# Reordering the stage between a projection and a mix: channel transform first, layer-norm sums among the time transform's parts

## The chip, the cores and the metric

The kernel runs on one core of one Trainium2 chip. The metric is the device time of one execution in microseconds (us), the median over the runs of the same program. All engine times below come from one profiled execution of it, in us from the start of its span.

## What is computed

The program is a transformer block (sliding-window attention and a squared-ReLU MLP), followed by a second model part of two layers on 1024 tokens and a context of 256. The change lies in the even layer of the second part, `_even_mix`, which all 1280 tokens pass:

```python
def _fourier_mix(v, fw):
    b, l, _ = v.shape
    vg = v.reshape(b, l, B_GROUPS, B_GROUP_DIM).astype(jnp.float32)
    f = jnp.fft.fftn(vg, axes=(1, 3), norm='ortho').real.astype(v.dtype)
    return jnp.einsum('blgd,gde->blge', f, fw).reshape(b, l, B_WIDTH)

def _even_mix(h, w_in, a_conv_w, a_conv_b, a_ln_g, a_ln_b, a_pw_w, a_pw_b, b_fw, w_out):
    a_val, a_glu, a_gate, b_val, b_gate = _split(h @ w_in, [A_WIDTH, A_WIDTH, A_WIDTH, B_WIDTH, B_WIDTH])
    u = a_val * jax.nn.sigmoid(a_glu)
    u = jax.nn.silu(_layernorm(_dwconv(u, a_conv_w) + a_conv_b, a_ln_g, a_ln_b))
    y_a = (u @ a_pw_w + a_pw_b) * jax.nn.silu(a_gate)
    y_b = _fourier_mix(b_val, b_fw) * jax.nn.silu(b_gate)
    return jnp.concatenate([y_a, y_b], axis=-1) @ w_out
```

`_dwconv` is a depthwise convolution of 31 taps. The Fourier transform over channels and time is done as matrix products.

## The kernel before, in words

Everything is float32. Each operand of a product is split into a rounded high part and a remainder, and `mm3` (lines 159 to 161) makes three matmuls out of one product: high by high, high by low, low by high. Activations lie with channels on the 128 partitions and tokens along the free side, in tiles of 512, 512 and 256 tokens (`TILES2`). Weights come as units of 512 KB through three slots: SyncE loads unit u once TensorE has begun unit u-2 (`load_unit`, line 138), ScalarE writes its high part (`split_hi`, line 149), VectorE its low part (`split_lo`, line 154). Each engine works through its own list strictly in the written order and waits on semaphores. A stage is a block; all engines meet at its end.

The even projection (the block that begins at line 1134) has 20 units of output channels. TensorE makes a unit's three tiles, ScalarE takes them out of PSUM (line 1152), and VectorE puts the convolution's taps between its other work: `taps(n, chunks)` issues `n` steps `conv_out = conv_in * w + conv_out` over 1295 columns (line 1252), in turn over the four channel chunks, 124 in all. The last four units are the Fourier branch: VectorE folds them (`fold`, lines 1222 to 1227), ScalarE writes `bH`, VectorE `bL` (`fold_low`, lines 1231 and 1232). ScalarE may take the next unit out only after `fold_low` of the last one.

The next block (from line 1310 on) is the stage of the change. Its jobs before the change, in TensorE's order:

- **Means:** 12 matmuls with a matrix of ones sum `conv_out` over channels (line 1333), three tiles by four chunks. VectorE subtracts the mean (`centred`, line 1478), ScalarE squares (line 1429, four buffers).
- **Channel transform:** ten blocks `z` of 12 matmuls each (`bH`, `bL` by `cdsH`, `cdsL`), in two pairs of banks in turn. ScalarE writes `zH` (line 1438), VectorE `zL` (line 1482). After each block one matmul sums squares (`square_sum`, line 1340).
- **Time transform:** four parts over the odd outputs, 24 matmuls of 512 columns each, then three halves of 48 matmuls of 256 columns each. Their outputs, `fH` and `fL`, are written by ScalarE (line 1463) and VectorE (line 1502) in four groups of four, alternating. The weights `wH`, `wL` are here constants of the transform.
- Beside it, the layer norm goes on: square root (ScalarE, line 1444), reciprocal (VectorE, line 1487), scaling by it (line 1491), silu and its high part (ScalarE, lines 1450 and 1452), low part (VectorE, line 1496). Each change between square root and silu on ScalarE has an `ACT_TABLE_LOAD`.
- **Mix:** 24 jobs of products with the Fourier weights and the pointwise weights, begun when `f_lo` is 16, each multiplied by its gate (lines 1521, 1523, 1468, 1510).

The waits that tie the time transform to the others, before:

```python
                    if half == 0:
                        pe.wait_ge(ln_rms, 3)
                    if half == 2:
                        pe.wait_ge(f_lo, 8)
```

## Time and profile before

| | us |
|---|---|
| median of 3 runs (lowest, highest) | 2329.1 (2325.64, 2332.3) |
| the profiled execution | 2324.8 |
| its span | 2323.0 |
| even projection's last matmul starts | 1444.58 |
| stage of the change, first matmul | 1460.06 |
| its channel transform starts | 1470.97 |
| its time transform starts | 1493.88 |
| its mix starts | 1539.62 |

TensorE (PE) is busy for 93% of the span, VectorE (DVE) for 56%, ScalarE (ACT) for 32%. The stage of the change is about 120 us of it. A line of the timeline gives start, duration, engine, source line and operation, output and inputs, and in brackets how long the engine sat idle before it and what released it. A matmul's duration is longer than the step to the next one, since they are pipelined; steps are read from the starts.

### The profile page before, as it was taken

The page shows a single profiled execution, that of the slowest core. Times are in us where ns is not written, and L with a number is a line of the kernel's source. Part 1 is how long each engine was busy: PE and PEld are TensorE (multiplying, and loading weights), DVE is VectorE, ACT ScalarE, POOL GpSimd, SP SyncE. Part 2 cuts the span into 40 slices and gives each one's busy share as a digit, 9 for nine tenths or more (in the row PEclk, how much of TensorE's full clock was granted, in tenths as well). Part 3 has the DMA queues.
Part 4 walks back from the last instruction along what each step waited for, and adds up shares of the span by engine and source line. Part 5 has one row for each costly group of instructions (what it writes and reads, how often), then busy time and mean ns, then how long its engine had stood idle before and what let it go on. Part 6 is the DMA issues. An engine that isn't in the chain of part 4 may idle for free. (4 is left out here: it accounts for less than half of the span.)

```text
span 2323.0 us, 25481 instructions
## 1 busy us (share of the span) xinstructions
PE 2159.5 (93%) x10132; PEld 1757.6 (76%) x10132; DVE 1299.4 (56%) x2157; ACT 733.4 (32%) x1366; POOL 196.4 (8%) x162
## 2 busy tenths in 40 slices
PE   5988989999999999999889998889989999879896
PEld 4876668788888888888578887678867788756675
DVE  6248853762462462464678888773354233478734
ACT  4236632420220220222441211651252211156522
POOL 2003310100000000000010000000020000044401
PEclk9978899999999999999989999899999999879998
DMA  4100021221221221221201231133121211100032
GB/s 152 55 19 1 1 91 55 106 103 54 98 102 55 99 101 55 100 100 55 109 28 37 71 91 39 51 102 138 40 119 46 82 46 55 36 5 15 10 118 82
DMA packets 42742, 157.95 MB, mean 68 GB/s; under 512 B 4224, under 2 KB 8960, under 8 KB 41344
## 3 DMA queue, kind: packets, MB, share of 16 engines
q1 hardware_dynamic: 40176, 146.49, 18.7%
q10 hardware_dynamic: 2448, 9.84, 1.1%
q8 instruction: 80, 1.31, 0.2%
q14 instruction: 38, 0.31, 0.0%
HBM read 136.39 MB, written 19.92 MB: 67 GB/s over the span
## 5 line engine op out<-in xcount | busy, mean ns | idle before, releaser
L159 PE MATMUL banks<-u2H,wH 128*128 128x512 f32 x736 | 291.6, 396 | 14.1 <-POOL u2L L355 5.0
L160 PE MATMUL banks<-u2L,wH 128*128 128x512 f32 x736 | 288.2, 392 | 0.0
L161 PE MATMUL banks<-u2H,wL 128*128 128x512 f32 x736 | 287.8, 391 | 0.0
L159 PE MATMUL banks<-uH,wH 128*128 128x512 f32 x672 | 262.8, 391 | 1.6 <-DVE uL L355 1.2
L154 DVE TENSOR_TENSOR wL<-raw,wH 128x1024 fp32r<-128x1024 f32 x153 | 186.8, 1222 | 138.3 <-ACT wH L149 138.3
L160 PE MATMUL banks<-uL,wH 128*128 128x512 f32 x672 | 262.4, 391 | 0.0
L161 PE MATMUL banks<-uH,wL 128*128 128x512 f32 x672 | 262.4, 390 | 0.0
L159 PE MATMUL banks<-aH,wH 128*128 128x512 f32 x640 | 249.7, 390 | 2.0 <-PEq L181 2.0
L160 PE MATMUL banks<-aL,wH 128*128 128x512 f32 x640 | 249.8, 390 | 0.0
L161 PE MATMUL banks<-aH,wL 128*128 128x512 f32 x640 | 249.7, 390 | 0.0
L149 ACT CAST wH<-raw 128x1024 fp32r<-128x1024 f32 x153 | 159.6, 1044 | 273.4 <-DMA raw<-in_wstream 268.5
L1252 DVE SCALAR_TENSOR_TENSOR conv_out<-conv_in,par,conv_out 128x1295 f32<-128x1295 f32 x120 | 180.3, 1562 | 0.6
L159 PEld LDWEIGHTS banks<-u2H,wH 128*128 128x128 f32 x736 | 139.1, 189 | 49.6 <-issue 16.0
L161 PEld LDWEIGHTS banks<-u2H,wL 128*128 128x128 f32 x736 | 139.0, 189 | 29.4
L160 PEld LDWEIGHTS banks<-u2L,wH 128*128 128x128 f32 x736 | 139.3, 189 | 28.8 <-issue 1.2
L1032 DVE TENSOR_TENSOR h<-banks,h 128x512 f32<-128x512 f32 x64 | 43.9, 689 | 206.6 <-PE banks L161 206.6
L159 PEld LDWEIGHTS banks<-uH,wH 128*128 128x128 f32 x672 | 126.8, 189 | 31.4 <-issue 5.1
L161 PEld LDWEIGHTS banks<-uH,wL 128*128 128x128 f32 x672 | 126.7, 189 | 26.5
L160 PEld LDWEIGHTS banks<-uL,wH 128*128 128x128 f32 x672 | 126.7, 189 | 26.2
L159 PEld LDWEIGHTS banks<-aH,wH 128*128 128x128 f32 x640 | 120.6, 188 | 27.4 <-issue 2.4
L161 PEld LDWEIGHTS banks<-aH,wL 128*128 128x128 f32 x640 | 120.6, 188 | 25.2
L160 PEld LDWEIGHTS banks<-aL,wH 128*128 128x128 f32 x640 | 120.4, 188 | 25.0
(277 smaller groups left out, 3802.0 us busy)
## 6 DMA issues: line engine op xcount, KB each, us to landing
raw<-in_wstream SPq DMA_DIRECT2D x153, 512.0 KB, 3.5
mod_w<-in_mod_w SPq DMA_DIRECT2D x48, 512.0 KB, 5.4
x_scratch<-h SPq DMA_DIRECT2D x2, 4096.0 KB, 11.3
gt<-gates_scratch SPq DMA_DIRECT2D x8, 640.0 KB, 4.1
h<-in_x SPq DMA_DIRECT2D x4, 1024.0 KB, 10.6
h<-in_x SPq DMA_DIRECT2D x1, 4096.0 KB, 13.4
h<-x_scratch SPq DMA_DIRECT2D x1, 4096.0 KB, 12.3
xo<-x_scratch SPq DMA_DIRECT2D x1, 4096.0 KB, 13.4
```

Of the source, the lines that this page charges most:

```text
L149: act.copy(wH[:, u % R, :], raw[:, u % R, :]).then_inc(weights_hi, 1)
L154: eng.tensor_tensor(wL[:, u % R, :], raw[:, u % R, :], wH[:, u % R, :].bitcast(F32), ALU.subtract)\
L159: first = pe.matmul(out, aH, bH, start=start, stop=False)
L160: pe.matmul(out, aH, bL, start=False, stop=False)
L161: return first, pe.matmul(out, aL, bH, start=False, stop=stop)
L1032: dve.tensor_tensor(dst, bank(4 + s * 2 + ti), dst, ALU.add).then_inc(down_drained, 1)
L1252: dve.scalar_tensor_tensor(dst, src, w, dst, ALU.mult, ALU.add).then_inc(conv_step, 1)
```

## The change

The taps: of the last two steps of the projection, the one that issued all taps that were left (11) now issues 4. The seven left over are issued in the next stage, four and three, between the splits of two weight units. `taps` moves out of the block and takes the engine as an argument. TensorE starts the stage with the channel transform; the means stand ahead of part `tc == 3` of the time transform and wait for all 124 taps; the square sums stand behind the groups of that part and of the first two halves. On ScalarE all twelve squares stand together ahead of the first group of outputs, and the square root and silu of each token tile stand between groups of outputs; on VectorE accordingly. Halves wait on other semaphores, some banks change.

```diff
@@ -1260,11 +1261,11 @@
                         if v < 8 and v % 2:
                             product(v // 2)
                         split_lo(dve, E0 + v + 2)
-                        taps(7, min((v + 1) // 2, HALF))
+                        taps(dve, 7, min((v + 1) // 2, HALF))
                     else:
                         fold(v - 16)
                         split_lo(dve, E0 + v + 2)
-                        taps(4 if v < 18 else HALF * TAPS, HALF)
+                        taps(dve, 4 if v < 19 else 0, HALF)
                         fold_low(v - 16)
...
@@ -1286,7 +1287,7 @@
...
-        Z_BANKS, MEAN_BANKS = (6, 0), (2, 5, 4)
+        Z_BANKS, MEAN_BANKS, SQ_BANKS = (6, 0), (1, 3, 5), (4, 5, 2)
...
-        ODD, MOD2, MOD0 = (6, 7, 2, 0), (4, 5), (1, 3)
+        ODD, MOD2, MOD0 = (6, 7, 2, 0), (1, 3), (6, 7)
...
@@ -1328,16 +1329,21 @@
...
-                for ti, (c0, n) in enumerate(STILES):
-                    for c in range(HALF):
-                        m = pe.matmul(bank(MEAN_BANKS[ti], n), ones[:], conv_out[:, c, c0:c0 + n], start=c == 0, stop=c == HALF - 1)
-                    m.then_inc(sum_done, 1)
+                def means():
+                    pe.wait_ge(conv_step, HALF * TAPS)
+                    for ti, (c0, n) in enumerate(STILES):
+                        for c in range(HALF):
+                            m = pe.matmul(bank(MEAN_BANKS[ti], n), ones[:], conv_out[:, c, c0:c0 + n], start=c == 0, stop=c == HALF - 1)
+                        m.then_inc(sum_done, 1)
+
...
                 def square_sum(j):
                     ti, c = jobs[j]
                     if j == HALF:
                         pe.wait_ge(centred, len(jobs))
+                    if j == 2 * HALF:
+                        pe.wait_ge(f_lo, 3)
                     pe.wait_ge(ln_sq_ready, j + 1)
-                    pe.matmul(bank(3 + ti, TILES2[ti][1]), ones[:], sq[:, j % LN_SQ, 0:TILES2[ti][1]], start=c == 0,
+                    pe.matmul(bank(SQ_BANKS[ti], TILES2[ti][1]), ones[:], sq[:, j % LN_SQ, 0:TILES2[ti][1]], start=c == 0,
                               stop=c == HALF - 1).then_inc(ln_sq_used, 1)
 
...
@@ -1351,10 +1357,6 @@
                             f.then_inc(units_begun, 1)
                         if g % 2:
                             m.then_inc(z_done, 1)
-                    if z >= 1:
-                        square_sum(z - 1)
-                for j in range(ZC - 1, len(jobs)):
-                    square_sum(j)
...
@@ -1362,6 +1364,8 @@
                     return u % R
                 D0 = W0["dft"]
                 for tc in range(4):
+                    if tc == 3:
+                        means()
                     slot = begin(D0 + tc)
...
@@ -1375,13 +1379,14 @@
                                 f.then_inc(units_begun, 1)
                         if tc == 3:
                             m.then_inc(dft_done, 1)
+                            square_sum(g)
                 for half in range(3):
                     u = D0 + 4 + min(half, 1)
                     slot = begin(u) if half < 2 else u % R
                     if half == 0:
-                        pe.wait_ge(ln_rms, 3)
-                    if half == 2:
-                        pe.wait_ge(f_lo, 8)
+                        pe.wait_ge(centred, 2 * HALF)
+                    else:
+                        pe.wait_ge(f_lo, (2, 8)[half - 1])
                     for g in range(HALF):
                         for tc in range(2):
                             for part in range(2):
@@ -1394,6 +1399,8 @@
                                 if g == 0 and tc == 0 and part == 0 and half < 2:
                                     f.then_inc(units_begun, 1)
                         m.then_inc(dft_done, 1)
+                        if half < 2:
+                            square_sum(HALF * (half + 1) + g)
 
                 for j, (_, _, bias, ti) in enumerate(mjobs):
                     oc, (c0, n) = j // 3, TILES2[ti]
...
@@ -1408,6 +1415,7 @@
                         pe.wait_ge(s_lo, len(jobs))
                     if j < 6:
                         pe.wait_ge(f_lo, 16)
+                        pe.wait_ge(ln_rms, 3)
                     else:
                         pe.wait_ge(mix_v, j - 5)
...
@@ -1428,41 +1436,57 @@
                         act.wait_ge(ln_sq_used, j - LN_SQ + 1)
                     act.activation(sq[:, j % LN_SQ, 0:n], conv_out[:, c, c0:c0 + n], ACT.Square).then_inc(ln_sq_ready, 1)
 
-                for s in range(2):
-                    act.wait_ge(gate_stored[s], 16 * 5)
-                for j in range(LN_SQ):
-                    square(j)
...
+                def root(ti):
+                    n = STILES[ti][1]
+                    act.wait_ge(ln_sq_used, (ti + 1) * HALF)
+                    act.activation(rs[:, TILES2[ti][0]:TILES2[ti][0] + n], bank(SQ_BANKS[ti], n), ACT.Sqrt, bias=eps[:, 0:1],
+                                   scale=1.0 / 512).then_inc(ln_rms, 1)
+
...
                 for z in range(ZC):
                     for half in range(2):
                         act.wait_ge(z_done, 2 * z + half + 1)
                         act.copy(zH[:, z, TN * half:TN * half + TN], bank(Z_BANKS[z % 2] + half)).then_inc(z_hi, 1)
-                    if z >= 1 and z - 1 + LN_SQ < len(jobs):
-                        square(z - 1 + LN_SQ)
-                split_hi(act, W0["dft"] + 2)
-                for ti, (c0, n) in enumerate(STILES):
-                    act.wait_ge(ln_sq_used, (ti + 1) * HALF)
-                    act.activation(rs[:, TILES2[ti][0]:TILES2[ti][0] + n], bank(3 + ti, n), ACT.Sqrt, bias=eps[:, 0:1], scale=1.0 / 512)\
-                        .then_inc(ln_rms, 1)
-                for j, (ti, c) in enumerate(jobs):
-                    c0, n = STILES[ti]
-                    v = conv_out[:, c, c0:c0 + n]
-                    act.wait_ge(ln_v, j + 1)
-                    act.activation(v, v, ACT.Silu, bias=pcol("ln_b", c)).then_inc(ln_silu, 1)
-                    act.wait_ge(ln_silu, j + 1)
-                    act.copy(sH[:, c, c0:c0 + n], v).then_inc(s_hi, 1)
-                    if j == 5:
-                        split_hi(act, W0["dft"] + 3)
+                    if z == 5:
+                        split_hi(act, W0["dft"] + 2)
+                split_hi(act, W0["dft"] + 3)
+                for s in range(2):
+                    act.wait_ge(gate_stored[s], 16 * 5)
                 split_hi(act, W0["dft"] + 4)
+                for j in range(len(jobs)):
+                    square(j)
+                spectrum(0)
                 split_hi(act, W0["dft"] + 5)
-                for j, (b, o, n, g, dst, scale) in enumerate(fjobs):
-
-
-                    act.wait_ge(dft_done, j + 1 if j < 4 or g % 2 else j + 2)
-                    if j >= 4 and g % 2:
-                        act.wait_ge(f_lo, j)
-                    act.activation(dst(fH, g), banks[:, b, o:o + n], ACT.Copy, scale=scale).then_inc(f_hi, 1)
-                    if j in (3, 7, 15):
-                        split_hi(act, W0["fw"] + (3, 7, 15).index(j))
+                root(0)
+                silu(0)
+                spectrum(4)
+                root(1)
+                silu(1)
+                split_hi(act, W0["fw"])
+                spectrum(8)
+                root(2)
+                silu(2)
+                split_hi(act, W0["pw"])
+                spectrum(12)
+                split_hi(act, W0["pw"] + 1)
                 for j, (yc, gc, bias, ti) in enumerate(mjobs):
                     act.wait_ge(mix_v, j + 1)
                     act.copy(tile_of(yH, yc, ti), gv[:, j % 3, 0:TILES2[ti][1]]).then_inc(y_hi, 1)
...
@@ -1471,38 +1495,64 @@
 
             @block.vector
             def _(dve):
...
                 split_lo(dve, W0["dft"] + 2)
-                for ti, (c0, n) in enumerate(STILES):
-                    dve.wait_ge(ln_rms, ti + 1)
-                    dve.reciprocal(rs[:, TILES2[ti][0]:TILES2[ti][0] + n], rs[:, TILES2[ti][0]:TILES2[ti][0] + n]).then_inc(ln_rstd, 1)
-                    dve.wait_ge(ln_rstd, ti + 1)
-                    for c in range(HALF):
-                        v = conv_out[:, c, c0:c0 + n]
-                        dve.scalar_tensor_tensor(v, v, pcol("ln_g", c), rs[:, TILES2[ti][0]:TILES2[ti][0] + n], ALU.mult, ALU.mult).then_inc(ln_v, 1)
+                taps(dve, 4, HALF)
                 split_lo(dve, W0["dft"] + 3)
-                for j, (ti, c) in enumerate(jobs):
-                    c0, n = STILES[ti]
-                    dve.wait_ge(s_hi, j + 1)
-                    dve.tensor_tensor(sL[:, c, c0:c0 + n], conv_out[:, c, c0:c0 + n], sH[:, c, c0:c0 + n].bitcast(F32),
-                                      ALU.subtract).then_inc(s_lo, 1)
+                taps(dve, HALF * TAPS, HALF)
+                for ti in range(2):
+                    centre(ti)
                 split_lo(dve, W0["dft"] + 4)
+                centre(2)
+                spectrum_low(0)
                 split_lo(dve, W0["dft"] + 5)
-                for j, (b, o, n, g, dst, scale) in enumerate(fjobs):
-                    dve.wait_ge(f_hi, j + 1)
-                    dve.scalar_tensor_tensor(dst(fL, g), banks[:, b, o:o + n], scale, dst(fH, g).bitcast(F32), ALU.mult,
-                                             ALU.subtract).then_inc(f_lo, 1)
-                    if j in (3, 7, 15):
-                        split_lo(dve, W0["fw"] + (3, 7, 15).index(j))
+                normalise(0)
+                spectrum_low(4)
+                normalise(1)
+                split_lo(dve, W0["fw"])
+                silu_low(0)
+                spectrum_low(8)
+                normalise(2)
+                silu_low(1)
+                split_lo(dve, W0["pw"])
+                spectrum_low(12)
+                silu_low(2)
+                split_lo(dve, W0["pw"] + 1)
 
```

`normalise(ti)` is the reciprocal and the four scalings of one tile, `silu_low(ti)` its four low parts, `spectrum_low(first)` the four `fL` of a group, `silu(ti)` four times silu and high part.

How the order moves, first on TensorE, at the third to fourth part of the time transform (`conv_out` by `ones` are the means, `wH` and `zH` the transform's operands):

```order
 L160 MATMUL banks<-wL,zH 128x512
 L161 MATMUL banks<-wH,zL 128x512
+L1336 MATMUL banks<-conv_out,ones 128x512 x8
+L1336 MATMUL banks<-conv_out,ones 128x256 x4
 L159 MATMUL banks<-wH,zH 128x512
 L160 MATMUL banks<-wL,zH 128x512
```

The 12 means are now behind 72 matmuls of the time transform instead of ahead of the channel transform, and the fourth part is behind them.

ScalarE before, from the last block of the channel transform on (`zH` is its high part, `ln_rs` the square root, `conv_out` the silu in place, `sH` its high part):

```order
L149 CAST wH<-raw 128x1024 [waits raw_loaded2]
L1444 ACT_TABLE_LOAD
L1444 ACTIVATE ln_rs<-banks,eps 128x512 [waits ln_sq_used] x2
L1444 ACTIVATE ln_rs<-banks,eps 128x256 [waits ln_sq_used]
L1450 ACT_TABLE_LOAD
L1450 ACTIVATE conv_out<-conv_out,par 128x512 [waits ln_v]
L1452 CAST sH<-conv_out 128x512 [waits ln_silu]
L1450 ACTIVATE conv_out<-conv_out,par 128x512 [waits ln_v]
```

and ScalarE of the change from the squares on (`ln_sq` squares, `fH` outputs of the time transform):

```order
L1437 ACTIVATE ln_sq<-conv_out 128x512 [waits ln_centred] x4
L1437 ACTIVATE ln_sq<-conv_out 128x512 [waits ln_sq_used,ln_centred] x4
L1437 ACTIVATE ln_sq<-conv_out 128x256 [waits ln_sq_used,ln_centred] x4
L1462 ACTIVATE fH<-banks 128x512 [waits dft_done] x4
L149 CAST wH<-raw 128x1024 [waits raw_loaded2]
L1442 ACT_TABLE_LOAD
L1442 ACTIVATE ln_rs<-banks,eps 128x512 [waits ln_sq_used]
L1450 ACT_TABLE_LOAD
L1450 ACTIVATE conv_out<-conv_out,par 128x512 [waits ln_v]
L1452 CAST sH<-conv_out 128x512 [waits ln_silu]
L1450 ACTIVATE conv_out<-conv_out,par 128x512 [waits ln_v]
L1452 CAST sH<-conv_out 128x512 [waits ln_silu]
```

The squares are no longer between the channel transform's blocks but in one row, each from the fifth on waiting for `ln_sq_used`, which TensorE's square sums raise; the first group of outputs stands behind them, then one tile's root and silu, and only then (three rows further) the second group of outputs. The same two table loads, root, silu and group follow twice more.

VectorE before, from the third tile's reciprocal on (`wL` weight unit's low part, `sL` low part of silu, `fL` low part of the outputs):

```order
L1487 RECIPROCAL ln_rs<-ln_rs 128x256 [waits ln_rms]
L1491 SCALAR_TENSOR_TENSOR conv_out<-conv_out,par,ln_rs 128x256 [waits ln_rstd]
L1491 SCALAR_TENSOR_TENSOR conv_out<-conv_out,par,ln_rs 128x256 x3
L154 TENSOR_TENSOR wL<-raw,wH 128x1024 [waits weights_hi]
L1496 TENSOR_TENSOR sL<-conv_out,sH 128x512 [waits ln_s_hi] x8
L1496 TENSOR_TENSOR sL<-conv_out,sH 128x256 [waits ln_s_hi] x4
L154 TENSOR_TENSOR wL<-raw,wH 128x1024 [waits weights_hi] x2
L1502 SCALAR_TENSOR_TENSOR fL<-banks,fH 128x512 [waits f_hi] x4
L154 TENSOR_TENSOR wL<-raw,wH 128x1024 [waits weights_hi]
L1502 SCALAR_TENSOR_TENSOR fL<-banks,fH 128x256 [waits f_hi] x4
```

and VectorE of the change, from the first group of outputs on:

```order
L1526 SCALAR_TENSOR_TENSOR fL<-banks,fH 128x512 [waits f_hi] x4
L154 TENSOR_TENSOR wL<-raw,wH 128x1024 [waits weights_hi]
L1509 RECIPROCAL ln_rs<-ln_rs 128x512 [waits ln_rms]
L1513 SCALAR_TENSOR_TENSOR conv_out<-conv_out,par,ln_rs 128x512 [waits ln_rstd]
L1513 SCALAR_TENSOR_TENSOR conv_out<-conv_out,par,ln_rs 128x512 x3
L1526 SCALAR_TENSOR_TENSOR fL<-banks,fH 128x256 [waits f_hi] x4
L1509 RECIPROCAL ln_rs<-ln_rs 128x512 [waits ln_rms]
L1513 SCALAR_TENSOR_TENSOR conv_out<-conv_out,par,ln_rs 128x512 [waits ln_rstd]
L1513 SCALAR_TENSOR_TENSOR conv_out<-conv_out,par,ln_rs 128x512 x3
L154 TENSOR_TENSOR wL<-raw,wH 128x1024 [waits weights_hi]
L1519 TENSOR_TENSOR sL<-conv_out,sH 128x512 [waits ln_s_hi] x4
L1526 SCALAR_TENSOR_TENSOR fL<-banks,fH 128x256 [waits f_hi] x4
```

Reciprocal and scaling of each tile now stand behind a group of `fL`, and a group of `fL` behind them, where before all three tiles were done ahead of all groups.

SyncE's list has the same transfers in the same order.

## Rows read from the trace of the kernel before

**Rows 1.** The page: engines over the span; DMA issues, KB each, us to landing.
```profile
PE 2159.5 (93%) x10132; PEld 1757.6 (76%) x10132; DVE 1299.4 (56%) x2157; ACT 733.4 (32%) x1366; POOL 196.4 (8%) x162
...
raw<-in_wstream SPq DMA_DIRECT2D x153, 512.0 KB, 3.5
```

**Rows 2.** Timeline of PE, 1444 to 1494: start us, us, instruction, [idle before <-releaser].
```profile
1444.58 0.28 PE L161 MATMUL banks<-u2Hc,wL 128*128 128x256 f32 x1
...
1460.06 11.26 PE L1333 MATMUL banks<-conv_out,ones 128*128 128x512 f32 x24 [15.20 <-PEq L1134]
...
1470.97 0.47 PE L159 MATMUL banks<-cdsH,bH 128*128 128x256 f32 x1
...
1478.62 1.02 PE L1340 MATMUL banks<-ln_sq,ones 128*128 128x512 f32 x2
...
1480.91 1.02 PE L1340 MATMUL banks<-ln_sq,ones 128*128 128x512 f32 x2
...
1492.34 1.89 PE L1340 MATMUL banks<-ln_sq,ones 128*128 128x256 f32 x8
```

**Rows 3.** Timeline of DVE around the end of the even projection.
```profile
1434.81 16.84 DVE L1252 SCALAR_TENSOR_TENSOR conv_out<-conv_in,par,conv_out 128x1295 f32<-128x1295 f32 x11
...
1454.55 0.69 DVE L1222 TENSOR_TENSOR bf<-bt 128x512 f32<-128x512 f32 x1 [1.43 <-ACT bt L1152]
...
1459.32 0.42 DVE L1232 TENSOR_TENSOR bL<-bt,bH 128x256 fp32r<-128x256 f32 x1
```

**Rows 4.** Timeline of ACT at the same place.
```profile
1453.16 1.36 ACT L1152 ACTIVATE bt<-banks 128x512 f32<-128x512 f32 x3 [18.01 <-DVE bL L1232]
```

**Rows 5.** Timeline of PE through the time transform, to the first mix matmul.
```profile
1493.88 0.59 PE L159 MATMUL banks<-wH,zH 128*128 128x512 f32 x1
...
1510.21 0.39 PE L161 MATMUL banks<-wH,zL 128*128 128x512 f32 x1
...
1512.83 0.79 PE L159 MATMUL banks<-wH,zH 128*128 128x512 f32 x1 [2.23 <-DVE wL L154]
...
1520.13 0.39 PE L159 MATMUL banks<-wH,zH 128*128 128x256 f32 x1
...
1537.38 0.28 PE L161 MATMUL banks<-wH,zL 128*128 128x256 f32 x1
...
1539.62 0.47 PE L159 MATMUL banks<-fH,wH 128*128 128x512 f32 x1 [1.96 <-DVE fL L1502]
```

**Rows 6.** Stretches: busy time of each engine, PEclk, DMA share, GB/s.
```profile
1514.00:1516.00 2.00, 2.00 (x7) 1.52 (x6) 2.00 (x4) 1.94 (x6) 0.00 (x0) 0.50 0.64 168
```

**Rows 7.** Timeline of DVE in the stage of the change.
```profile
1478.72 1.41 DVE L1482 TENSOR_TENSOR zL<-banks,zH 128x512 fp32r<-128x512 f32 x2 [0.88 <-ACT zH L1438]
...
1496.11 3.35 DVE L1487 RECIPROCAL ln_rs<-ln_rs 128x512 f32<-128x512 f32 x1 [0.78 <-ACT ln_rs L1444]
...
1499.49 2.74 DVE L1491 SCALAR_TENSOR_TENSOR conv_out<-conv_out,par,ln_rs 128x512 f32<-128x512 f32 x4
...
1512.69 6.25 DVE L1496 TENSOR_TENSOR sL<-conv_out,sH 128x512 fp32r<-128x512 f32 x12
...
1518.86 2.35 DVE L154 TENSOR_TENSOR wL<-raw,wH 128x1024 fp32r<-128x1024 f32 x2
```

**Rows 8.** Timeline of ACT in the stage of the change.
```profile
1494.09 1.28 ACT L1444 ACT_TABLE_LOAD   x1
...
1495.38 1.63 ACT L1444 ACTIVATE ln_rs<-banks,eps 128x512 f32<-128x512 f32 x3
...
1497.03 1.28 ACT L1450 ACT_TABLE_LOAD   x1
...
1500.28 0.73 ACT L1450 ACTIVATE conv_out<-conv_out,par 128x512 f32<-128x512 f32 x1 [1.96 <-DVE conv_out L1491]
...
1501.56 0.72 ACT L1450 ACTIVATE conv_out<-conv_out,par 128x512 f32<-128x512 f32 x1
...
1525.06 0.63 ACT L1463 ACTIVATE fH<-banks 128x256 fp32r<-128x256 f32 x1
...
1528.98 0.64 ACT L1463 ACTIVATE fH<-banks 128x256 fp32r<-128x256 f32 x1 [0.80 <-DVE fL L1502]
```

81 lines of the change are left out of this document (59 added, 22 removed).

## The prediction

> **What bounds the kernel now.** On the page TensorE is busy for 93% of the span [rows 1], so time is lost only where it waits. I read its timeline first, for gaps. The largest in this stretch lies before the stage of the change: the last matmul of the projection starts at 1444.58, the first of the stage at 1460.06, with 15.2 us idle in brackets [rows 2]. VectorE's timeline shows why: it issues 11 taps in a row from 1434.81, 16.84 us [rows 3]; ScalarE may not take out the last unit before, and its bracket shows 18.01 us of waiting [rows 4]; then fold and low part end at 1459.74, which is 1459.32 + 0.42 [rows 3]. Behind the gap TensorE makes the means, 10.91 us (1460.06 to 1470.97), and the channel transform with the squares, 22.91 us (to 1493.88) [rows 2, 5]. The time transform has three short gaps: 2.4 us before its fourth part, 0.2 before the halves, 2.1 before the mix (steps from the last start: 1510.21 to 1512.83, and 1537.38 to 1539.62, less one matmul) [rows 5]. Gaps up to the mix: 15.4 + 2.4 + 0.2 + 2.1 = 20.1 us. After a gap of 2.4 us the granted clock is 0.50, 1.2 instead of 2.4 GHz [rows 6], and the fourth part takes 7.30 us (1512.83 to 1520.13) for the work of one of the first three, 16.33 x 72/71 / 3 = 5.5 [rows 5]: 1.6 lost with the 0.2 gap taken off. What VectorE and ScalarE do costs nothing as long as it fits beside that; so I read their timelines for how long each job takes [rows 7, 8].
>
> **The rates.** A matmul of 512 columns steps 0.23 us (1493.88 to 1510.21 holds 72), one of 256 steps 0.12 (1520.13 to 1537.38 holds 144) [rows 5]. A block of the channel transform with one square sum steps 2.29 (1478.62 to 1480.91) [rows 2], so a sum costs 2.29 - 12 x 0.12 = 0.85, one of 256 columns half. The 12 means at full clock: 8 x 0.85 + 4 x 0.43 = 8.5; they took 10.9, so 2.4 went to the clock after the long gap. A tap is 16.84/11 = 1.53 [rows 3]. On VectorE a reciprocal and four scalings of 512 take 3.38 + 2.66 = 6.0, a low part 0.62, a weight split 1.15 [rows 7]. On ScalarE a table load is 1.28, a root 0.6, silu with high part 1.28 (1500.28 to 1501.56) [rows 8]. A group of four outputs, handed to and fro between ScalarE and VectorE, takes 3.9 from its first to its last start [rows 8].
>
> **The stage's start: 9.1 us earlier.** With 4 instead of 11 taps the third fold's low part ends about 10.7 earlier, before TensorE has made the last tile; ScalarE then waits for that tile (1444.70), its last piece takes 0.4 to 0.6, and the fold starts near 1445.4 instead of 1454.55 [rows 3, 4]. The rest of the tail is kept: 5.2 + 0.3 us to the first matmul. TensorE starts at 1451.0.
>
> **Channel transform.** Ten blocks of 1.44 are 14.4. The first 4.8 us run at half clock, 2.4 more (as for the means). VectorE needs 1.41 per block [rows 7], which is just under TensorE's 1.44, and ScalarE has one weight split among its copies: 1.1 for small waits. End at 1468.9, 25.0 us ahead of the old 1493.9.
>
> **Parts one to three, then the means.** 72 matmuls end at 1485.3. Meanwhile VectorE ends its low parts (1470.3), does a split, four taps (to 1477.5), then waits for the split of unit dft+3. That unit is requested when part two begins (1474.4), lands 3.5 later [rows 1], and ScalarE rounds it by 1479.5. So VectorE waits 2.0, splits, and ends the last three taps at 1485.3, just as TensorE arrives; the margin is zero. Means 8.5, to 1493.8. Fourth part and its four sums 5.45 + 3.4, to 1502.6. First half with four sums 5.8 + 3.4, to 1511.8.
>
> **What is late next.** ScalarE's list has all twelve squares ahead of the first output. The last one needs the eighth square sum, which stands at the end of the first half. Only then come: square, four outputs, split of unit dft+5 (0.3 + 2.3 + 1.0), VectorE's split 1.2. TensorE needs that unit for the second half and waits 5.1 us, to 1516.9. The second half with its sums is 7.6, and 1.3 for the clock, to 1526.2. The third half needs the second group's `f_lo`, and ScalarE has the first tile's root and silu ahead of it: load and root 1.9, reciprocal and first scaling 4.1, four silus 5.3, group 3.9: 15.1 from 1515.6, then the last low part. TensorE waits 5.2 more, to 1531.4, and ends at 1538.9 (5.8 + 1.8 for the clock). All its transform work is then done, but the mix waits for all 16 `f_lo`. The second tile has the same 15.1, and in it a weight split on each engine and four low parts of silu ahead of the third group, 4.0: from 1530.6 to 1549.7. The third tile has 256 tokens and its columns cost half: load and root 1.7, reciprocal and first scaling 2.3, silus 3.5, splits 2.1, last group about 2.8: to 1562.0. TensorE waits 23.1 us. Before, the same work ran under parts two to four, and three groups in a row cost only 2.1.
>
> **The sum.** TensorE does the same matmuls, so only gaps and clock count. Gaps: 6.3 + 1.1 + 5.1 + 5.2 + 23.1 = 40.8 against 20.1: +20.7. Clock: 2.4 + 1.3 + 1.8 = 5.5 against 2.4 + 1.6 = 4.0: +1.5. The mix itself keeps its waits (its second weight unit still lands after its begin); I give 0.3 for a colder start. (This is bookkeeping: the clock on the two halves costs nothing by itself, since it only shortens the wait behind them. What sets the mix's start is the chain.) Together **+22.5 us**, the mix starting at 1562.0 instead of 1539.62. Stepping the old order with the same rates gives the old start of the mix within 0.1 us, so I trust the steps to a few us, not the rates only. The profiled execution was 2324.8, so it becomes 2347.3; the median of the runs shown is 4.3 higher at 2329.1, which gives 2351.6. I say 2351.
>
> Four table loads are added. In the trace the root starts at 1495.38, right when the load of 1494.09 ends, and the next load starts right behind the third root [rows 8]: 1.28 is the whole price. Two of the four lie on the chain (2.6), the two before silu under the reciprocal. The Trainium skill, "ScalarE: Activation LUTs", section "What ACT_TABLE_LOAD costs", speaks against this change: each switch to another set costs the load and about 1.38 us of drain, 2.66 in all. By that rule the two loads on the chain would give 2.8 more and the sum would be +25.3; the rows show no such drain, so it stays out.
>
> **Unknown costs.** Two prices are not in the trace. The means' wait for the last tap has no margin: a landing of 4.6 rather than 3.5 adds 1.1; a shorter one gains nothing, since TensorE arrives at 1485.3 anyway. The hand-overs between engines, some 30 on the last chain, are costed at 0.04 each; at 0.08 it is 2 more, and where queued instructions overlap better, 3 less. Together 2346 to 2356.
>
> **Rivals.** *It packs.* VectorE and ScalarE find their inputs ready, and only VectorE's work behind the last square counts: three reciprocals with scalings 15.4 (1496.11 to the split before 1512.69), low parts of silu 4.9 before the last group, three splits 3.5, 16 low parts of outputs 8.2: 32 us from 1512, mix at 1544, +4.5: 2334. For it: VectorE is busy only 56% [rows 1]. Against: root, reciprocal and silu of a tile need each other, and each tile stands behind the group before it.
>
> *TensorE sets the end* (faster). Then the mix starts when its own list ends: 1451.0 + 17.9 + 16.4 + 8.5 + 8.9 + 9.2 + 7.5 + 5.8 = 1525.2, 14.4 earlier: 2315. It decides if the work behind the last square fits beside the 13 us of the last two halves. For it: the 9.1 at the stage's start and the means' clock loss are really gone. Against: that chain is 50 us by the rows.
>
> **Chances.** A measurement of this kernel can tell about 0.3%, 7 us, from no change. My forecast has 0.88, packing 0.05 (at 2334 it is near that bound: 0.03 same, 0.02 slower), TensorE's end 0.04, something unseen 0.03 (0.01 same, 0.02 slower). So slower 0.88 + 0.02 + 0.02 = 0.92, same 0.04, faster 0.04. The range takes the forecast's bounds and half the way to packing: 2342; above it, the bounds and 3 us for what the steps miss: 2359.
>
> **What would show it.** The profile of the changed kernel should show: the first channel matmul about 9 us earlier and the time transform's first 25 us earlier; a gap of some 5 us before the second half, released by a weight split; one of 5 before the third, released by `fL`; one of 20 to 25 before the mix, released by `fL`; six table loads in the stage. If the gap before the mix is under 10 us, the chain argument is wrong; if the means wait for taps by more than 2 us, the unit's landing was mis-sized.

## The result, and the profile after

| | before | after |
|---|---|---|
| median of 5 runs (lowest, highest), us | 2329.1 (2325.64, 2332.3) | 2350.42 (2343.75, 2352.74) |
| profiled execution, us | 2324.8 | 2348.87 |
| its span, us | 2323.0 | 2347.1 |

The changed kernel takes 1.0088 times as long, 95% interval 1.0069 to 1.0107: 21 us more by the medians, 24.1 by the spans of the two profiled executions. (The median before is that of five executions, not of three.) The page of the changed kernel:

```profile
PE 2163.2 (92%) x10132; PEld 1761.3 (75%) x10132; DVE 1299.7 (55%) x2157; ACT 738.3 (31%) x1370; POOL 196.7 (8%) x162
```

TensorE is busy for 3.7 us longer than before [rows 1]; all else is idle time. (A mean or a square sum, in plain float32, stands in the trace as two records: `x24` are the 12 means.) The timeline of PE of the changed kernel shows where, at the borders of each piece of the stage (columns as in [rows 2]):

```profile
1445.14 0.28 PE L161 MATMUL banks<-u2Hc,wL 128*128 128x256 f32 x1
1451.39 0.55 PE L159 MATMUL banks<-cdsH,bH 128*128 128x256 f32 x1 [5.96 <-PEq L1156]
...
1468.97 0.50 PE L159 MATMUL banks<-wH,zH 128*128 128x512 f32 x1
...
1485.53 8.86 PE L1336 MATMUL banks<-conv_out,ones 128*128 128x512 f32 x24
1494.04 0.59 PE L159 MATMUL banks<-wH,zH 128*128 128x512 f32 x1
...
1517.26 0.58 PE L159 MATMUL banks<-wH,zH 128*128 128x256 f32 x1 [4.77 <-DVE wL L154]
...
1525.64 0.59 PE L1346 MATMUL banks<-ln_sq,ones 128*128 128x256 f32 x2
1531.77 0.58 PE L159 MATMUL banks<-wH,zH 128*128 128x256 f32 x1 [5.53 <-DVE fL L1526]
...
1539.88 0.28 PE L161 MATMUL banks<-wH,zL 128*128 128x256 f32 x1
1562.65 0.77 PE L159 MATMUL banks<-fH,wH 128*128 128x512 f32 x1 [22.50 <-DVE fL L1526]
```

The stage begins 6.25 us behind the projection's last matmul instead of 15.48 [rows 2], and the time transform begins at 1468.97 instead of 1493.88. The means take 8.51 us (1485.53 to 1494.04); before, behind the long gap, 10.91 [rows 2]. Then come three gaps: 4.77 us before the second half, 5.53 before the third, 22.50 before the mix, the last two released by `fL`. Before there were 2.23 ahead of the fourth part and 1.96 ahead of the mix [rows 5]. The last transform matmul starts at 1539.88, where before the mix itself began at 1539.62. From its first matmul to the mix, the time transform takes 93.7 us (1468.97 to 1562.65) instead of 45.7, 48 more: 8.5 for the means and about 8.5 for the square sums, which have only moved into it, 28.6 more of gaps, and some 2.4 more to the clock. So most of the 25 us by which the time transform begins earlier is moved work; the real gain, at the stage's start, is 9 us.

The timeline of ACT of the changed kernel shows the chain on which these gaps stand:

```profile
1512.59 0.42 ACT L1437 ACTIVATE ln_sq<-conv_out 128x256 f32<-128x256 f32 x1 [1.87 <-PE banks L1346]
1512.91 2.12 ACT L1462 ACTIVATE fH<-banks 128x512 fp32r<-128x512 f32 x4
1514.88 1.07 ACT L149 CAST wH<-raw 128x1024 fp32r<-128x1024 f32 x1
1515.96 1.28 ACT L1442 ACT_TABLE_LOAD   x1
1517.26 0.69 ACT L1442 ACTIVATE ln_rs<-banks,eps 128x512 f32<-128x512 f32 x1
1517.96 1.28 ACT L1450 ACT_TABLE_LOAD   x1
1522.15 0.72 ACT L1450 ACTIVATE conv_out<-conv_out,par 128x512 f32<-128x512 f32 x1 [2.90 <-DVE conv_out L1513]
...
1531.10 1.28 ACT L1442 ACT_TABLE_LOAD   x1
...
1543.35 0.62 ACT L1462 ACTIVATE fH<-banks 128x256 fp32r<-128x256 f32 x1
1547.72 1.07 ACT L1462 ACTIVATE fH<-banks 128x256 fp32r<-128x256 f32 x2 [3.75 <-DVE fL L1526]
...
1550.22 1.28 ACT L1442 ACT_TABLE_LOAD   x1
```

From the sixth on, each square waits for a square sum of TensorE (1.87 in the bracket of the last), and the first four outputs (`fH`, 1512.91) stand behind all twelve squares; TensorE had them ready ten us earlier, at the end of the fourth part. A split, a table load and a root follow, then silu waits for VectorE. The first group of outputs of the halves is done at 1531.08, and only then may the next root begin. The row at 1547.72 shows the two lists locking each other: ScalarE waits 3.75 us for an `fL`, because VectorE has other work in front of it. The timeline of DVE of the changed kernel:

```profile
1479.56 1.23 DVE L154 TENSOR_TENSOR wL<-raw,wH 128x1024 fp32r<-128x1024 f32 x1 [2.04 <-ACT wH L149]
1480.71 4.77 DVE L1150 SCALAR_TENSOR_TENSOR conv_out<-conv_in,par,conv_out 128x1295 f32<-128x1295 f32 x3
...
1531.11 0.61 DVE L1526 SCALAR_TENSOR_TENSOR fL<-banks,fH 128x256 fp32r<-128x256 f32 x1 [0.74 <-ACT fH L1462]
1533.11 3.35 DVE L1509 RECIPROCAL ln_rs<-ln_rs 128x512 f32<-128x512 f32 x1 [1.40 <-ACT ln_rs L1442]
...
1543.48 1.23 DVE L154 TENSOR_TENSOR wL<-raw,wH 128x1024 fp32r<-128x1024 f32 x1 [4.23 <-ACT wH L149]
1544.62 2.50 DVE L1519 TENSOR_TENSOR sL<-conv_out,sH 128x512 fp32r<-128x512 f32 x4
1547.03 0.60 DVE L1526 SCALAR_TENSOR_TENSOR fL<-banks,fH 128x256 fp32r<-128x256 f32 x1
...
1550.23 0.60 DVE L1526 SCALAR_TENSOR_TENSOR fL<-banks,fH 128x256 fp32r<-128x256 f32 x1 [0.74 <-ACT fH L1462]
...
1562.13 0.42 DVE L1526 SCALAR_TENSOR_TENSOR fL<-banks,fH 128x256 fp32r<-128x256 f32 x1 [0.51 <-ACT fH L1462]
```

VectorE stands 4.23 us at 1543.48 for `wH`, which ScalarE writes behind its four silus; then it splits, makes four low parts of silu (1544.62), and only at 1547.03 the `fL` that ScalarE waits for. The last `fL` ends at 1562.55, and the mix starts 0.10 later. From the first `fL` (1513.54) to that end VectorE is busy for 32.6 us of 49.0. Its work alone, which the prediction's rival *It packs* put at 32, does not fill the time; 16.4 us of it is waiting.

**A measure for the stage.** The part of the program ahead of the stage, and the part behind it, vary by some us from one execution to another, which is as much as some of the experiments move. So I read in each trace two marks: E, the start of the last projection matmul, and N, SyncE's first load of the block behind the mix. These are N before and N after (the timeline of SP, of the two kernels):

```profile
1583.13 0.32 SPq L1538 DMA_DIRECT2D h<-x_scratch  x1
```

```profile
1606.44 0.32 SPq L1588 DMA_DIRECT2D h<-x_scratch  x1
```

| kernel | E | first matmul | mix | N | E to mix | mix to N | E to N |
|---|---|---|---|---|---|---|---|
| before | 1444.58 | 1460.06 | 1539.62 | 1583.13 | 95.04 | 43.51 | 138.55 |
| after | 1445.14 | 1451.39 | 1562.65 | 1606.44 | 117.51 | 43.79 | 161.30 |
| e1, squares split | 1445.40 | 1451.64 | 1560.40 | 1604.21 | 115.00 | 43.81 | 158.81 |
| e2, norm behind | 1446.16 | 1452.40 | 1537.95 | 1596.70 | 91.79 | 58.75 | 150.54 |
| e3, roots together | 1442.19 | 1448.43 | 1563.29 | 1606.95 | 121.10 | 43.66 | 164.76 |
| e4, taps only | 1446.43 | 1463.66 | 1542.69 | 1586.51 | 96.26 | 43.82 | 140.08 |
| e5, one split in before | 1440.72 | 1456.19 | 1536.21 | 1577.77 | 95.49 | 41.56 | 137.05 |
| e6, packed order | 1442.67 | 1448.91 | 1531.99 | 1575.63 | 89.32 | 43.64 | 132.96 |
| e7, packed order, split | 1448.52 | 1454.76 | 1537.71 | 1579.72 | 89.19 | 42.01 | 131.20 |

(One of e6's twelve executions was slow, 5145.32 us at a granted clock of 1.0 and with no cause known, and is not in its ratio below.) The change makes the stage 22.75 us longer (161.30 less 138.55). The rest of the 24.1 is 0.56 ahead of E and 0.79 behind N; of the change only the shorter row of taps reaches ahead of E, and nothing lies behind N.

### The profile page after: what moved, and what is told of

It reads as the page before. It is cut to its first block and busy times, and to the rows that moved or that the text cites. A ratio compares the mean times of both kernels' runs of the same rounds, so it can differ in the third digit from the quotient of the medians.

```text
span 2347.1 us, 25487 instructions
## 1 busy us (share of the span) xinstructions
PE 2163.2 (92%) x10132; PEld 1761.3 (75%) x10132; DVE 1299.7 (55%) x2157; ACT 738.3 (31%) x1370; POOL 196.7 (8%) x162
## 5 line engine op out<-in xcount | busy, mean ns | idle before, releaser
L159 PEld LDWEIGHTS banks<-uH,wH 128*128 128x128 f32 x672 | 126.8, 189 | 31.6 <-issue 5.1
```

Of the source, the lines that this page charges most:

```text
L159: first = pe.matmul(out, aH, bH, start=start, stop=False)
```

## The experiments

The theory is that of the prediction: the gaps follow from the order of the lists of ScalarE and VectorE behind the last square. The rivals were that the new place of the taps and means costs the time, that single items on the lists cost it (table loads, squares), or that VectorE's total work does. e1, e3 and e4 were executed once each, e2 seven times, e5 and e6 twelve times, e7 six times. The marks of every kernel come from one trace.

### e1: four squares behind the first group of outputs

```diff
-                for j in range(len(jobs)):
+                for j in range(2 * HALF):
                     square(j)
                 spectrum(0)
                 split_hi(act, W0["dft"] + 5)
+                for j in range(2 * HALF, len(jobs)):
+                    square(j)
```

> The changed kernel with ScalarE's last four squares moved behind the first group of outputs and the split of unit dft+5. Theory (a chain through ScalarE and VectorE sets the mix's start, TensorE's gaps are only its shadow): the gap of 4.8 us before the second half goes away, the gap before the third half grows from 5.5 to about 9, the gap before the mix stays at 22, and the mix starts about 3 us earlier relative to the start of the stage's first matmul (108.2 us behind it instead of 111.3). Rival (each gap of TensorE is a cost of its own, as my bookkeeping sum reads): removing the gap brings its whole 4.8 us and the clock loss of 1.3 behind it, so the mix starts 105 us behind the first matmul.

Measured: 2346.56 us. The gap before the second half is gone; these two are left in PE's timeline of e1:

```profile
1529.53 0.58 PE L159 MATMUL banks<-wH,zH 128*128 128x256 f32 x1 [8.90 <-DVE fL L1528]
...
1560.40 0.76 PE L159 MATMUL banks<-fH,wH 128*128 128x512 f32 x1 [22.44 <-DVE fL L1528]
```

The mix starts 108.8 us behind the stage's first matmul; the theory said 108.2, the rival 105. The outputs and the weight split no longer wait for the squares, so TensorE's 4.77 us gap vanishes, but most of it comes back as a longer gap before the third half (8.90 for 5.53). Only 2.5 us reach N. A gap of TensorE is worth something only if it lies on the chain, and this one lay beside it.

### e2: the whole normalising behind all outputs

```diff
                 spectrum(0)
                 split_hi(act, W0["dft"] + 5)
-                root(0)
-                silu(0)
                 spectrum(4)
-                root(1)
-                silu(1)
                 split_hi(act, W0["fw"])
                 spectrum(8)
-                root(2)
-                silu(2)
                 split_hi(act, W0["pw"])
                 spectrum(12)
+                for ti in range(3):
+                    root(ti)
+                for ti in range(3):
+                    silu(ti)
                 split_hi(act, W0["pw"] + 1)
```

VectorE's list is changed in the same way.

> The changed kernel with roots, reciprocals, silus and their low parts of all three tiles behind all four groups of outputs. Theory (the mix starts late because each group stands behind a tile's layer norm): the mix starts some 85 us behind the stage's first matmul instead of 111, 26 us less. Its gap of 22.5 before the mix falls to about 4 and is released by the roots. But the layer norm is then late for the pointwise half of the mix: TensorE waits about 17 us there, and the whole is only 10 to 11 us faster than the changed kernel, 12 slower than before. Rival (the chain is not what holds the mix; VectorE's amount of work is): the mix start hardly moves, under 5 us, and the total stays at 2350.

Measured: 2339.13 us median, 1.0041 times before, interval 1.0025 to 1.0057. PE's timeline of e2:

```profile
1537.95 0.77 PE L159 MATMUL banks<-fH,wH 128*128 128x512 f32 x1 [4.44 <-ACT ln_rs L1442]
...
1560.47 0.77 PE L159 MATMUL banks<-fH,wH 128*128 128x512 f32 x1 [16.86 <-DVE gv L1567]
```

The mix starts 85.55 us behind the stage's first matmul, 25.7 earlier than in the changed kernel. So neither the taps nor the means nor the square sums cause the two late gaps: all three have the same places here, and the last output is done 1.8 us behind TensorE's last transform matmul (1533.51 to 1535.32). Only the gap before the second half, 4.77 us, is still there, since its weight split still stands behind the squares. The two late gaps shrink by 23.6 us. But the work is not gone: it now lies behind the outputs, and the pointwise products wait 16.86 us for it. The edit also takes some 21 us of VectorE's work out from ahead of the last output, and the stage has two table loads instead of six; so e2 alone does not tell the order of the lists from the amount of work in them. That is what e6 is for. In the stage, 10.8 us of the 22.75 are won back, and 12.0 remain.

### e3: the three roots together, two table loads instead of six

```diff
-                root(0)
+                for ti in range(3):
+                    root(ti)
                 silu(0)
                 spectrum(4)
-                root(1)
                 silu(1)
                 split_hi(act, W0["fw"])
                 spectrum(8)
-                root(2)
                 silu(2)
```

> The changed kernel with the three roots together ahead of the first silu, so that the stage has two table loads instead of six. Theory (order of the chain decides, and a root must not wait for the last square sum): the first tile's root now waits for nothing new but the second and third root wait for square sums of the second half, so silu and the second group come later; the mix starts about 4 us later than in the changed kernel, 115 us behind the stage's first matmul, although four table loads are gone. Rival (table loads set the chain's length; with the drain that the notes give, 2.66 us each): the mix starts 5 to 10 us earlier, 101 to 106 us behind.

The drain that the text speaks of is that of the Trainium skill, "ScalarE: Activation LUTs", section "What ACT_TABLE_LOAD costs". Measured: 2345.99 us. The timelines of ACT and PE of e3:

```profile
1523.79 0.47 ACT L1442 ACTIVATE ln_rs<-banks,eps 128x256 f32<-128x256 f32 x1 [7.80 <-PE banks L1346]
1524.28 1.28 ACT L1450 ACT_TABLE_LOAD   x1
1525.57 0.72 ACT L1450 ACTIVATE conv_out<-conv_out,par 128x512 f32<-128x512 f32 x1
```

```profile
1535.19 0.58 PE L159 MATMUL banks<-wH,zH 128*128 128x256 f32 x1 [11.44 <-DVE fL L1525]
...
1563.29 0.77 PE L159 MATMUL banks<-fH,wH 128*128 128x512 f32 x1 [20.80 <-issue]
```

Four loads fewer, and the mix starts 114.86 us behind the first matmul, 3.6 later than in the changed kernel. The third root needs the last square sum, which TensorE makes at the end of the second half; ScalarE stands 7.80 us in front of it, and the first tile's silu and the second group of outputs stand behind. The stage is 3.5 us longer; the total is a little lower only because the parts ahead of E and behind N ran quicker in this execution, by 3.0 and 3.4 us. What the loads are worth can still be read: from the first silu to the mix e3 takes 37.72 us (1525.57 to 1563.29), the changed kernel 40.50 (1522.15 to 1562.65). Two later roots with their loads are gone from that stretch, for 2.8 us, close to the 2.6 that the prediction gave the loads on the chain. No drain shows here either: the silu starts 0.01 us behind the end of its load. So the loads are a small part of the 22.75, and taking them away at the price of a wait of 7.80 is a loss.

### e4: the taps alone, in the kernel before

The projection issues 4 taps at its end, as in the change; the seven left over stand ahead of the means, which stay where they were. (`taps` also moves out of its block, as in the change; not shown.)

```diff
-                        taps(4 if v < 18 else HALF * TAPS, HALF)
+                        taps(dve, 4 if v < 19 else 0, HALF)
...
+                pe.wait_ge(conv_step, HALF * TAPS)
                 for ti, (c0, n) in enumerate(STILES):
...
+                taps(dve, HALF * TAPS, HALF)
```

> The kernel before with only the taps of the change: seven taps issued at the start of the stage, everything else as before, the means first on TensorE and waiting for them. Theory (the 9 us at the stage's start are real only where TensorE has other work than the means): the block starts 9 us earlier, TensorE then waits some 10 us more for the taps, the means start at about 1462, and the mix starts about 2 us later than before, total +2. Rival (the shorter tail of the projection is a gain by itself): the means start near 1452 to 1455 and the total is 5 to 9 us under the kernel before.

Measured: 2330.5 us in its one execution, beside a median of 2328.46 of the kernel before. The timelines of DVE and PE of e4:

```profile
1452.67 10.94 DVE L1150 SCALAR_TENSOR_TENSOR conv_out<-conv_in,par,conv_out 128x1295 f32<-128x1295 f32 x7 [0.32 <-PEq L1156]
```

```profile
1463.66 10.76 PE L1335 MATMUL banks<-conv_out,ones 128*128 128x512 f32 x24 [16.95 <-DVE conv_out L1150]
```

The seven taps start at once, but TensorE waits for their end: it starts 17.23 us behind E instead of 15.48. The stage is 1.5 us longer. Moving the taps gains nothing by itself; the channel transform must take their place ahead of the means. That part of the change is right, and it brought its 9 us.

### e5: one weight split moved, in the kernel before

```diff
-                    if j in (3, 7, 15):
-                        split_lo(dve, W0["fw"] + (3, 7, 15).index(j))
+                    if j in (3, 7):
+                        split_lo(dve, W0["fw"] + (3, 7).index(j))
...
+                    if j == 6:
+                        split_lo(dve, W0["pw"] + 1)
```

> The kernel before, with one edit: VectorE's low part of the second pointwise unit (1.2 us) moves from behind the sixteenth output of the transform into the mix, behind its job 6. Its high part stays where it is. My theory (the last waits of a stage are where a queued instruction counts): the mix starts where it did, about 79.6 us behind the stage's first matmul, the wait of some 2 us that TensorE has early in the mix for the list of VectorE is gone, and the total is about 2 us below the kernel before. Rival A, the split is hidden: no difference (within 0.5 us). Rival B, the split late in the mix makes the pointwise products wait for it: 1 to 3 us longer.

Measured: 2324.78 us median beside 2327.93 of the kernel before, ratio 0.999, interval 0.9979 to 1.0. PE's timeline of e5, early in the mix:

```profile
1543.07 0.36 PE L159 MATMUL banks<-fH,wH 128*128 128x256 f32 x1 [0.19 <-DVE gv L1521]
...
1544.27 0.47 PE L159 MATMUL banks<-fH,wH 128*128 128x512 f32 x1 [0.61 <-DVE gv L1521]
```

The mix starts 95.49 us behind E, 0.45 later than before, and from there to N it takes 41.56 us instead of 43.51. The stage gains 1.5 us, the median 2 to 3. By the interval alone this is hardly told from nothing. The marks say more: in the six traces with this split in its old place (e2, with its wait in the mix, left out), mix to N is 43.51 to 43.82.

### e6: the change's start with the lists packed anew

ScalarE's list, from its first square on:

```python
                for j in range(0, 6):
                    square(j)
                split_hi(act, W0["dft"] + 4)
                split_hi(act, W0["dft"] + 5)
                root(0)
                for j in range(6, 7):
                    square(j)
                spectrum(0)
                for j in range(7, 12):
                    square(j)
                root(1)
                spectrum(4)
                split_hi(act, W0["fw"])
                root(2)
                silu(0)
                silu(1)
                spectrum(8)
                spectrum(12)
                split_hi(act, W0["pw"])
                silu(2)
                split_hi(act, W0["pw"] + 1)
```

VectorE issues all seven taps between the splits of units dft+2 and dft+3. Later it has the outputs' low parts 0 to 3, the first tile's normalising, low parts 4 to 7, the second tile's, a split, the third tile's. The square sums stand earlier: six behind groups of the fourth part instead of four, and the last behind the second half's first group instead of its fourth.

> Keeps the change's start (channel transform first, seven taps behind it) and orders the rest anew: all taps ahead of the weight splits, squares and square sums as early as the time transform's fourth part and first two halves allow, the three roots one by one ahead of all silus (two table loads instead of six), and the spectrum's first groups ahead of the normalising. The theory (the loss is the order of the lists on ScalarE and VectorE behind the last square, not the new place of the taps): the first channel matmul stays near 1451, the mix starts about 82.6 us behind it (1533.6, against 1539.6 in the kernel before and 1562.7 in the change) after one wait of some 9 us, and the total is about 6 us below the kernel before, 2323. Rival A (any order that puts the square sums among the parts leaves the same chain): mix at 1550 or later, 2335 or more. Rival B (unseen hand-overs): mix at 1540, total as before.

Measured: 2323.5 us median, 0.9978 times before, interval 0.9969 to 0.9987. The timelines of PE and ACT of e6:

```profile
1531.99 0.77 PE L159 MATMUL banks<-fH,wH 128*128 128x512 f32 x1 [9.17 <-issue]
...
1539.31 0.47 PE L159 MATMUL banks<-fH,wH 128*128 128x512 f32 x1 [1.95 <-DVE gv L1577]
```

```profile
1512.79 0.48 ACT L1445 ACTIVATE ln_rs<-banks,eps 128x256 f32<-128x256 f32 x1
1513.29 1.28 ACT L1453 ACT_TABLE_LOAD   x1
...
1524.28 0.62 ACT L1455 CAST sH<-conv_out 128x512 fp32r<-128x512 f32 x1
1524.81 0.63 ACT L1465 ACTIVATE fH<-banks 128x256 fp32r<-128x256 f32 x1
```

and of DVE, its last output:

```profile
1531.46 0.42 DVE L1533 SCALAR_TENSOR_TENSOR fL<-banks,fH 128x256 fp32r<-128x256 f32 x1 [0.51 <-ACT fH L1465]
```

The third root ends at 1513.27 and one silu load follows; eight silus with their high parts run without a gap from 1514.58 to 1524.81, and the outputs follow at once. The mix starts 83.1 us behind the first matmul, expected 82.6, after one gap of 9.17 (the trace names no releaser for it, but the last `fL` ends 0.11 us ahead of it). The stage is 28.3 us shorter than in the changed kernel and 5.6 shorter than before, expected 6.

VectorE's timeline shows where the 28.2 us come from by which the mix now starts closer to the stage's first matmul (83.1 for 111.3). In e6 its first `fL` starts 51.4 us behind the stage's first matmul (1500.27), in the changed kernel 62.2: 10.8 us. From there to the end of the last `fL` it takes 31.6 us, of which 27.5 busy, against 49.0, of which 32.6 busy: 12.3 us less waiting, and 5.1 less work ahead of the last output, since one group of silu's low parts and two splits now stand elsewhere. So VectorE's work is now nearly all of the chain, as the rival *It packs* has it. The matmuls, the squares and VectorE's items are the same in number, but three things changed at once: the order of the lists, the places of the square sums, and two table loads instead of six. The loads alone are worth some 3 us by e3; order and places are not told apart by a run.

### e7: both

e6 with the edit of e5.

> The packed order, with VectorE's low part of the second pointwise unit moved into the mix behind job 6 as well. If both effects are separate they add: mix start as in the packed order, and 1.5 to 2 us less in all, about 7.5 us below the kernel before (2321). Rival: the mix of the packed order starts with other work still queued on VectorE, so that the split hides there anyway, and this is no faster than the packed order alone.

Measured: 2318.8 us median beside 2327.93 of the kernel before, ratio 0.9959, interval 0.9947 to 0.9971. PE's timeline of e7:

```profile
1537.71 0.77 PE L159 MATMUL banks<-fH,wH 128*128 128x512 f32 x1 [9.14 <-issue]
...
1543.23 0.47 PE L159 MATMUL banks<-fH,wH 128*128 128x512 f32 x1 [0.20 <-DVE gv L1576]
```

The stage is 7.35 us shorter than before; e5 and e6 alone gave 1.5 and 5.6, which add up to 7.1. From the mix to N it takes 42.01 us (e6: 43.64), with 0.20 us of waiting where e6 has 1.95. The split was not hidden in the packed order either. This version beats both kernels, that before by 0.4%.

## Why the prediction was right, point by point

| step | predicted | measured |
|---|---|---|
| median of the kernel | 2351 (2342 to 2359) | 2350.42 |
| first matmul of the stage | 1451.0 | 1451.39 |
| time transform starts | 1468.9 | 1468.97 |
| last tap ends | 1485.3 | 1485.48 |
| means | 1485.3 to 1493.8 | 1485.53 to 1494.04 |
| gap before the second half | 5.1 | 4.77 |
| second half starts, ends | 1516.9, 1526.2 | 1517.26, 1526.24 |
| gap before the third half | 5.2 | 5.53 |
| third half starts, ends | 1531.4, 1538.9 | 1531.77, 1540.15 |
| first, second and third tile's chain | 15.1, 19.1, 12.3 | 15.1, 19.1, 12.3 |
| gap before the mix | 23.1 | 22.50 |
| mix starts | 1562.0 | 1562.65 |
| E to N, more than before | 22.5 | 22.75 |

(A gap's end less its bracket gives where the work before it ended. The tiles' chains run from one root's table load to the next, 1515.96, 1531.10 and 1550.22, the third to the last low part's end, 1562.55.)

- **The start.** E lay 0.56 later in this execution. From E to the first matmul it took 6.25 us, predicted 6.4. The projection's last unit was taken out by ScalarE at 1445.46, as soon as TensorE had made it.
- **The taps' zero margin.** VectorE waited 2.04 us for its split, predicted 2.0, and its last tap ended 0.05 us ahead of the means' first matmul. The landing that the rows of before gave was right: ScalarE had the unit rounded at 1479.53, predicted 1479.5.
- **The chain.** It held at every link: root behind the load, reciprocal and scaling, silus, outputs handed to and fro. e2 fits it: without the normalising between the outputs, the gaps before the third half and the mix shrink from 28 us to 4.4. And VectorE's 16.4 us of waiting inside the chain are what its work alone cannot explain.
- **The table loads.** The root starts at 1517.26, right behind its load (1515.96 + 1.28 = 1517.24), and the load for silu at 1517.96, right behind the root (1517.26 + 0.69 = 1517.95). No drain is to be seen ahead of any of the six or behind the three root loads; behind the three silu loads ScalarE waits for VectorE here, but in e3 and e6 a silu starts right behind its load (e6: 1513.29 + 1.28 = 1514.57, the next silu at 1514.58). By the Trainium skill's rule with a drain, which the prediction works out, the stage would have been 25.3 us longer, not 22.75. e3 does not show that loads are free: it took four away and put a wait of 7.80 us in their place.
- **The clock.** The two halves behind gaps lost 1.4 and 2.6 us to it, predicted 1.3 and 1.8; the channel transform lost 1.8, predicted 2.4. As the prediction said, this is bookkeeping: the third half ended 1.25 us later than predicted and the gap behind it was shorter by 0.6, the mix moved by 0.65, of which 0.39 is there at the stage's start.
- **The mix itself.** It costs 0.28 us more (43.79 for 43.51), predicted 0.3.
- **The rivals.** *It packs* put the mix at 1544; that needs other lists, and e6 shows that they exist: its mix starts 83.1 us behind the first matmul, which is 1534.5 for a stage that starts where that of the changed kernel does. So VectorE's work does fit once the order lets it, and its price of 32 us was right (32.6 busy in the changed kernel); the prediction gave this rival too little thought as a thing one could build, though it was right that this change doesn't do it. *TensorE sets the end* is refuted by the 22.50 us gap.
- **Luck.** That the median came within 0.6 us of 2351 is luck in part: the executions of the changed kernel alone lie between 2343.75 and 2352.74. The marks are the better test: E to N agrees within 0.3, although single pieces are off by up to 1.25 (the third half's end).
- **What the prediction did not carry.** Its unknown costs (+1.1, +2, -3) around 2351 make 2348 to 2354, not 2346 to 2356; no term carries the rest. That stepping the old order gives the old start of the mix within 0.1 us is said and not worked out. Steps made for the experiments stand better: from first matmul to mix they said 108.2, 85, 115 and 82.6 for e1, e2, e3 and e6, and 108.8, 85.6, 114.9 and 83.1 were measured.

## What to carry to other kernels

An engine that works through a written list pays for the order of the list, not only for its work: when one stage's outputs and another stage's chain of root, reciprocal and activation share two engines, each item put between outputs delays every output behind it, and a wait of one engine for the other repeats at every exchange. Before a stage is moved to fill a gap, step the lists of the other engines to the point where all of its work must be done; here 9 us won at the start were followed by 33 us of waits where there had been 4, and the same start with the lists in another order (and four table loads fewer) was worth 5.6 us against the kernel before. A gap that is removed is worth only what the next wait doesn't take: of 4.8 us of gap in e1, 2.5 arrived.

## What the runs showed that I had not expected

- After gaps of nearly the same length the granted clock stayed at 0.50 for different times. The stretches of the changed kernel (columns: window, length, busy time and instructions of each engine, PEclk, DMA share, GB/s):

```profile
1520.00:1522.00 2.00, 2.00 (x16) 1.95 (x16) 1.97 (x2) 0.00 (x0) 0.00 (x0) 0.96 0.42 166
1534.00:1536.00 2.00, 2.00 (x12) 2.00 (x11) 2.00 (x1) 0.38 (x1) 0.00 (x0) 0.50 0.00 0
1566.00:1568.00 2.00, 2.00 (x6) 1.61 (x6) 0.01 (x1) 1.04 (x1) 0.00 (x0) 0.51 0.16 64
```

After the gap of 4.77 us the clock is back by about 1520, 3 us behind the first matmul; after that of 5.53 us matmuls step 0.21 instead of 0.12 until 1537.06, 5.3 us. The third half lost 1.2 us more than the second by this alone.
- After the 22.50 us of waiting the mix runs at 0.50 for its first 5 us (the last stretch above), and still costs only 0.28 us more than before. The kernel before had waited only 1.96 us there, and its mix ran at half clock too, twice (stretches of before):

```profile
1540.00:1542.00 2.00, 2.00 (x7) 1.51 (x6) 0.00 (x0) 0.00 (x0) 0.00 (x0) 0.51 0.40 113
1548.00:1550.00 2.00, 2.00 (x8) 1.71 (x7) 2.00 (x5) 0.90 (x2) 0.00 (x0) 0.50 0.36 67
```

So the long gap cost no more clock than the short one did, and TensorE's waits inside the mix sum to 2.8 us in both.
- Over the nine traces E lies between 1440.72 and 1448.52, though the program ahead of it is the same but for the number of taps at its end. A difference of a few us in the total of one execution says nothing about a stage; two marks around the stage do.
- The seven taps cost 1.56 us each in the new block (10.94 for 7), and 1.53 in the old one [rows 3]: their place hardly changes their price.
